# Input split in place in the first block; the first gates in three passes behind the pool projection, with the sample's values between its chunks

## What is computed

```python
z = rms_norm(x) @ w_in   # u 512 | q 512 | k 256 | v 256 | qi 256 | ki 64 | wi 4 | gates 2048
a_pool = pool_mixer(u)   # trailing windows 2, 4, 8, 16, per-group map
a_attn = attend(q, the 256 keys of the highest indexer score, their values, rel_bias)
g = sigmoid(gates)
m = g[..., :1024] * (a_pool @ w_pool_proj) + g[..., 1024:] * (a_attn @ w_attn_proj)
h = x + m @ w_out
y = rms_norm(h + (silu(f[..., :2816]) * f[..., 2816:]) @ w_down), f = rms_norm(h) @ w_gate_up
```

## Time and profile before

| | |
|---|---|
| time of the profiled execution, own time | 1810.34 us |
| its span, first to last instruction | 1808.6 us |
| mean granted TensorE clock, share of 2.4 GHz | 0.975 |
| PE busy (matmuls) | 1689.4 us, 93% |
| DVE (VectorE) busy | 767.3 us, 42% |
| ACT (ScalarE) busy | 458.3 us, 25% |
| POOL (GpSimd) busy | 407.0 us, 23% |

### The profile page before, as it was taken

The page is one execution under the profiler, slowest core; times in us unless marked ns, Lnnn a source line. Parts: engine busy times, 40 slices in busy tenths (PEclk is TensorE's granted clock), DMA queues, the critical chain, the costliest instruction groups (busy, mean ns, idle before and its releaser), DMA issues.

```text
span 1808.6 us, 25066 instructions
## 1 busy us (share of the span) xinstructions
PE 1689.4 (93%) x9820; PEld 1407.8 (78%) x9820; DVE 767.3 (42%) x1882; ACT 458.3 (25%) x860; POOL 407.0 (23%) x351
## 2 busy tenths in 40 slices
PE   4998699989999898779999999999999999999997
PEld 2554266646666555568889999999999999999996
DVE  2214899999200455342144443313313313313325
ACT  1213211253112554331133321121121121121113
POOL 3000205411111432011112242232232232232220
PEclk9996899999999899989999999999999999999999
DMA  5500411260111332032221121111111111111002
GB/s 156 113 26 1 153 63 36 79 247 18 35 38 38 140 141 94 13 100 59 66 70 47 60 81 47 47 46 46 46 46 46 46 46 46 46 46 46 0 1 106
DMA packets 114687, 116.91 MB, mean 65 GB/s; under 512 B 17310, under 2 KB 103982, under 8 KB 112557
## 3 DMA queue, kind: packets, MB, share of 16 engines
q1 hardware_dynamic: 102471, 73.74, 13.7%
q0 software_dynamic: 4160, 39.33, 6.5%
q10 hardware_dynamic: 7982, 2.83, 0.6%
HBM read 107.66 MB, written 8.45 MB: 64 GB/s over the span
## 4 chain that ended last, share of the span: by engine, by line
PE 55%; DVE 1%; DMA 1%; ACT 1%; issue 0%; DVEq 0%; ACTq 0%
PE banks L108 52%; PE banks L1538 3%; DMA out_dram<-yo 0%; PE banks L1519 0%; DVE yo L1856 0%; DVE XL L1769 0%; DMA raw<-in_w_in_dram 0%; ACT XH L1682 0%; DVE rinv L1821 0%; ACT junk L1759 0%; ACT hT L1679 0%; ACT sH L1673 0%; PE banks L1615 0%; PE banks L1561 0%; DVE gated L1776 0%
## 5 line engine op out<-in xcount | busy, mean ns | idle before, releaser
L108 PE MATMUL banks<-hnH,wH 128*128 128x344 f32 x1056 | 339.0, 321 | 3.8 <-DVE sg L1830 3.8
L108 PE MATMUL banks<-hnH,wL 128*128 128x344 f32 x1056 | 337.8, 320 | 0.0
L494 PE MATMUL banks<-hT,big 128*128 128x344 f32 x768 | 226.9, 457 | 1.3 <-ACT I L977 0.7
L494 PEld LDWEIGHTS banks<-hT,big 128*128 128x128 f32 x768 | 147.3, 192 | 79.0 <-issue 2.4
L108 PEld LDWEIGHTS banks<-hnH,wH 128*128 128x128 f32 x1056 | 199.4, 189 | 4.4 <-issue 4.3
L1647 POOL TENSOR_TENSOR wL<-w_raw,wH 128x1024 fp32r<-128x1024 f32 (+1 forms) x55 | 155.8, 2851 | 204.2 <-ACT wH L1709 203.9
L108 PEld LDWEIGHTS banks<-hnH,wL 128*128 128x128 f32 x1056 | 199.2, 189 | 0.0
L1844 DVE TENSOR_TENSOR hT<-hT,banks 128x344 f32<-128x344 f32 x264 | 135.2, 513 | 107.1 <-PE banks L108 107.0
L108 PE MATMUL banks<-aH,wH 128*128 128x344 f32 x528 | 169.3, 321 | 1.6 <-DVE hT L1844 1.6
L108 PE MATMUL banks<-aH,wL 128*128 128x344 f32 x528 | 169.7, 321 | 0.0
L108 PE MATMUL banks<-hnL_lo,wH 128*128 128x344 f32 x528 | 169.1, 320 | 0.0
(11 more groups left out here) (287 smaller groups left out, 2621.1 us busy)
## 6 DMA issues: line engine op xcount, KB each, us to landing
w_raw<-in_w_gate_up_dram SPq DMA_DIRECT2D x44, 512.0 KB, 3.9
w_raw<-in_w_down_dram SPq DMA_DIRECT2D x11, 1024.0 KB, 4.9
big<-in_w_in_dram SPq DMA_DIRECT2D x12, 512.0 KB, 3.9
W<-in_x_prompt_dram SPq DMA_DIRECT2D x8, 512.0 KB, 4.5
raw<-in_w_in_dram SPq DMA_DIRECT2D x8, 512.0 KB, 5.0
x_nat<-in_x_prompt_dram SPq DMA_DIRECT2D x8, 512.0 KB, 4.0
raw<-in_w_out_dram SPq DMA_DIRECT2D x8, 512.0 KB, 3.8
out_dram<-yo SPq DMA_DIRECT2D x8, 512.0 KB, 2.6
```

The costliest lines, as they stand in the source:

```text
L108: last = nc.tensor.matmul(out, w_cols(w, k), x_cols(x, k), start=(k == 0 and j == 0), stop=(k == nk - 1 and j == 2))
L494: last = mm(ps[:, bank, 0:CH], big[:, s, k, :], hT[:, k, c * CH:(c + 1) * CH], start=k == 0, stop=k == KD - 1)
```

## The change

- The area `UD` moves next to `hT`. `XH`, the input's high part, replaces `hT` in place, piece by piece; `XL` lies over `UD`. `x_hi` holds a piece's high part for the while. The residual gets an area of its own in the second block.
- PE does all 24 chunks of the pool projection first, then all first gates, in three passes, on slabs that ACT and POOL split (`high_slab`, `low_slab`). POOL splits the first 12 pieces of the input beside the projections, VectorE the last 12 after them.
- The sample's values lie between the projection's chunks 8 to 23, in 16 halves, each of two `rc`; the gather and its ring are in halves.
- VectorE's loops are three: blocks 3, 4, 5; then the sample and block 2; then blocks 6 and 7, with the sample's softmax steps after rounds 18, 22 and 25.
- PE takes `sum_sample_ties` ahead of the cached keys and waits there; the masks of the sample are added as matmuls at the end of the key stage.
- In attention `transpose_probs(n)` comes after `times_values(n - 1)`.
- In the second block the input's split is gone; the first projection slab and two transposes of x come before the first gate slab, and SP's loads are in another order.

```diff
+                pe.wait_ge(sm_step, SM["ties"])
+                pe.wait_ge(upto_made, 1)
+                mm(ps[:, 6, 0:P + 2], same16[:, :, :].rearrange("p b r -> p (b r)"), seq[:, :], start=True, stop=True)
+                mm(ps[:, 6, 256:256 + P + 1], upto16[:, :], seq[:, 0:P + 1], start=True, stop=True).then_inc(sm_made, 1)
                 pe.wait_ge(zq_ready, 1)
                 pe.wait_ge(uq_evac, 6 + 24)
                 pe.wait_ge(stT_evac, 1)
...
+                pe.wait_ge(sm_step, SM["mask"])
+                pe.wait_ge(lanes_made, 10)
+                for j in range(2):
+                    for b4 in range(4):
+                        for g in range(2):
+                            mm(ps[0:32, 2, j:j + 1], ZQ[:, g, j, 32 * b4:32 * b4 + 32], kT[:, g, SEQ + 4 * j + b4:SEQ + 4 * j + b4 + 1],
+                               start=(b4 == 0 and g == 0), stop=False)
+                    mm(ps[0:32, 2, j:j + 1], new_sel[:, j, :], MK[:, P:P + 1], start=False, stop=True)
+                    for c in range(4):
+                        for rc in range(4):
+                            last = mm(ps[32 * rc:32 * rc + 32, 4 + j, c * P:(c + 1) * P], lane_sel[:, j, c, 32 * rc:32 * rc + 32], MK[:, 0:P],
+                                      start=False, stop=c == 3, tile_position=(0, 32 * rc))
                 last.then_inc(S_ready, 1)
...
+                def sample_values(h):
+                    b, s = divmod(h, 2)
+                    j = b // 4
+                    pe.wait_ge(v_in[s], 16 * (b + 1))
+                    if b == 0:
+                        pe.wait_ge(sp_evac, 2)
+                    elif s == 0:
+                        pe.wait_ge(ob_done, b)
+                    for rc in (2 * s, 2 * s + 1):
+                        for c in range(4):
+                            at = (4 * (rc % 2) + c) * 256
+                            last = mm(ps[32 * rc:32 * rc + 32, 7, 0:256], PTs[:, j, c, 32 * rc:32 * rc + 32], v_ring[:, s, at:at + 256],
+                                      start=c == 0, stop=c == 3 and rc > 0, tile_position=(0, 32 * rc))
+                        if rc == 0:
+                            mm(ps[0:32, 7, 0:256], pd[:, 32 * j:32 * j + 32], vN[0:NB, NBLK, :], start=False, stop=True, tile_position=(0, 0))
+                    last.then_inc(v_used, 1)
...
+                transpose_max()
+                beside = {1: transpose_negmax, 3: sum_probs, 5: transpose_sample_probs}
+                for x in range(PROJ):
+                    m, c = divmod(x, NCH)
+                    if c == 0:
+                        pe.wait_ge(small_in[m % 2], 16 * (m // 2 + 1))
+                    if x >= 6:
+                        pe.wait_ge(p_evac, x - 5)
+                    for k in range(4):
+                        last = mm(ps[:, x % 6, 0:CH], small[:, m % 2, k, :], aP[:, k, c * CH:(c + 1) * CH], start=k == 0, stop=k == 3)
+                    last.then_inc(p_ready, 1)
+                    if x in beside:
+                        beside[x]()
+                    if x >= V_FROM:
+                        h = x - V_FROM
+                        if h >= 2 and h % 2 == 0:
+                            sum_sample_heads(h // 2 - 1)
+                        sample_values(h)
+                sum_sample_heads(NB - 1)
...
                 for m in range(KD):
                     s = m % 2
...
+                    pe.wait_ge(slab_lo, m + 1)
                     for c in range(NCH):
...
+                        for a, k in enumerate(G_ORDER):
+                            if m == 0 and a == 0:
+                                pe.wait_ge(xh_done, 4 * (c + 1))
+                            if m == 0 and a >= 4:
+                                pe.wait_ge(xh_done, 4 * (NCH + c) + a - 3)
+                            for j, (w, v) in enumerate((("hi", "hi"), ("hi", "lo"), ("lo", "hi"))):
+                                last = mm(ps[:, x % 6, 0:CH], G_[w][s][:, k * P:(k + 1) * P], X_[v][:, k, chunk(c)],
+                                          start=(a == 0 and j == 0), stop=(a == KD - 1 and j == 2))
...
                     if n and n % 4 == 0:
                         transpose_sums(n // 4 - 1)
                     if n:
                         times_values(n - 1)
-                    if n in VF_AT:
-                        sum_sample_heads(VF_AT.index(n))
-                    if n in V_AT:
-                        sample_values(V_AT.index(n))
+                    transpose_probs(n)
                 times_values(PAIRS - 1)
...
+                pool.wait_ge(S_ready, 1)
+                load_v(0)
+                load_v(1)
+                for u in range(12):
+                    c, k = units[u]
+                    if u == 0:
+                        pool.wait_ge(ap_ready, NG * NCH)
+                    pool.wait_ge(split_hi, u + 1)
+                    gp.tensor_tensor(XL[:, k, chunk(c)], hT[:, k, chunk(c)], f32(x_hi[u % 2]), ALU.subtract).then_inc(split_lo, 1)
+                    if u >= 2:
+                        load_v(u)
+                for h in range(12, 2 * NB):
+                    load_v(h)
+                low_slab(0)
+                low_slab(1)
                 for m in range(KD):
...
+                dve.wait_ge(causal_done, 4)
...
+                    for c, i in enumerate((3, 4, 5)):
+                        count(c, i, cntA[:, c:c + 1])
...
+                    count(0, 2, cntB[:, 32:33])
+                    dve.wait_ge(lane_step, 4 * r + 1)
+                    V.transpose(lane_cntT[:, :], lane_cnt[:, :]).then_inc(lane_step, 1)
+                    dve.wait_ge(lane_step, 4 * r + 2)
+                    V.tensor_reduce(lane_tot[:, :], lane_cntT[:, :].rearrange("p (b r) -> p b r", r=16), AX.X, ALU.add).then_inc(lane_step, 1)
+                    dve.wait_ge(lane_step, 4 * r + 3)
+                    V.tensor_copy(lane_totT[:, :].rearrange("p (b r) -> p b r", r=16),
+                                  lane_tot[:, :].unsqueeze(2).to_broadcast([P, 2, 16])).then_inc(lane_step, 1)
                     dve.wait_ge(lane_step, 4 * r + 4)
                     V.transpose(cntB[:, 0:32], lane_totT[:, :]).then_inc(counted, 1)
-                    dve.wait_ge(counted, 3 * BITS + 4 * (r + 1))
-                    update(LATER, cntB[:, 31:35], bit, 2 * BITS + 1 + 2 * r)
-                settle(LATER, 4 * BITS + 1)
+                    dve.wait_ge(counted, 3 * BITS + 2 * (r + 1))
...
+                sample_step = {18: sample_max, 22: sample_negmax, 25: sample_weights}
+                LAST = slice(5, 7)
+                for r, bit in enumerate(range(BITS - 1, -1, -1)):
+                    for c, i in enumerate((6, 7)):
+                        count(c, i, cntA[:, c:c + 1])
+                    dve.wait_ge(counted, 5 * BITS + 2 * (r + 1))
+                    update(LAST, cntA[:, 0:2], bit, 4 * BITS + 2 + 2 * r)
+                    if r in sample_step:
+                        sample_step[r]()
+                settle(LAST, 6 * BITS + 2)
+                for k, i in ((4, 6), (5, 7)):
+                    to_mask(k, i)
...
+                dve.wait_ge(p_ready, PROJ)
+                for u in range(12, 24):
+                    c, k = units[u]
+                    dve.wait_ge(split_hi, u + 1)
+                    V.tensor_tensor(XL[:, k, chunk(c)], hT[:, k, chunk(c)], f32(x_hi[u % 2]), ALU.subtract).then_inc(split_lo, 1)
...
-                slab(0)
-                slab(1)
...
                     if m < 2:
+                        slab(m)
                         x_tile(m)
...
+                project(0)
+                for m in range(KD):
+                    if m == 0:
+                        for t in transpose_after(0):
+                            transpose_x(t)
+                    gate(m)
+                    if m:
+                        project(m)
+                        for t in transpose_after(m):
+                            transpose_x(t)
...
-                for n, (c, k) in enumerate(order):
-                    A(XH[:, k, chunk(c)], hT[:, k, chunk(c)], ACT.Copy).then_inc(split_hi, 1)
-                    if n == KD:
-                        high_slab(1)
+                high_slab(1)
+                for t in transpose_after(0):
+                    x_out(t)
...
+                def high_x(u):
+                    c, k = units[u]
+                    if u >= 2:
+                        act.wait_ge(xh_done, u - 1)
+                    A(x_hi[u % 2], hT[:, k, chunk(c)], ACT.Copy).then_inc(split_hi, 1)
+                def keep_x(u):
+                    c, k = units[u]
+                    act.wait_ge(split_lo, u + 1)
+                    A(XH[:, k, chunk(c)], f32(x_hi[u % 2]), ACT.Copy).then_inc(xh_done, 1)
...
+                    if 6 <= x < 18:
+                        high_x(x - 6)
+                        if x > 6:
+                            keep_x(x - 7)
+                    if x > V_FROM and x % 2:
+                        own_values((x - V_FROM) // 2)
+                    if x > V_FROM + 1 and x % 2 == 0:
```

(34 more changed lines are left out.)

444 lines of the change are left out of this document (192 added, 252 removed).

## The result

The changed kernel takes **1858.3 us** (median of 4 runs, 1856.07 to 1861.8) against 1810.99 for the kernel before in the same measurement: ratio 1.0259, 95% interval 1.0243 to 1.0274. It is slower by 47.3 us; forecast were 53.

The account below looks back on a forecast made before the run. TensorE, busy for 93% of the span, was taken as the bound. Terms -20.4 + 2.0 + 39.9 + 22.2 + 2.4 + 1.0 + 10 - 7.7 + 4.0 = +53.4 us gave 1864, range 1834 to 1886.

Parts of the forecast that it names:

- the sample's values: Value products between the projections: eight samples take 59.2 us instead of 19.3 at the serial price, +39.9 us.
- wait for the ties: Ahead of the cached keys: PE idles 24.1 us for VectorE's ties, slowed by POOL, where it idled 1.9; +22.2 us.
- low clock after it, masks as narrow products: Key stage: low clock after the ties pause +2.4 us, masks as 32 narrow products for 8 wide ones +1.0.
- the softmax waits: First projections: PE waits 6 us for sample_negmax and 4 us for sample_weights, +10 (4 to 16); sample_max is covered.
- attention, values and head sums aside: Attention: start wait shrinks -2.6, VectorE waits in the transposes go -6.0, last times_values +0.9; sum -7.7 us.
- second block's start: Second block: SP's load order and ACT's split ahead of the x copy delay the first gate slab, +4.0 us (-5 to +6).
- one column group behind each other, then four on the next: Sample's values: products run serially at 0.48 us each, less some 0.4 at each group change; 7.4 us a sample.
- The first rival: Sample's values: the two column groups of a half overlap, a sample costs 3.95 us; 1836 us, chance 0.12.
- The rival with VectorE in time: Ties ahead of the keys: POOL does not hold VectorE's short steps, the wait is 1 us; 1840 us, chance 0.07.
- its two waits, 3.3 and 2.7 us, go: Attention's transposes: with times_values ahead, VectorE has emptied its bank, so PE's waits for it vanish; -6.0 us.
- The rival at 1960: Value stage: narrow products leave PE mostly idle, the clock falls to 1.2 GHz, 59 + 37 us double; chance 0.05.
- the one on the fast side: Value products run beside the projections at no PE cost; under 5.8 us the sum turns negative, at nothing 1805; chance 0.04.

Follow-up runs that it names:

- ties_and_steps: Changed kernel with PE's two ties products moved into the key loop and VectorE's sample softmax steps after rounds 9, 11, 13 instead of 18, 22, 25: 1828.26 us.
- rc_inside: Changed kernel with the value products' columns c outside, the half's two row groups inside, and the new token's product behind all eight: 1838.99 us.
- mixer_late: Changed kernel with one more wait on POOL, so the pool mixer starts only after VectorE has done the sample's ties: 1882.67 us in one run.
- ties_in_keys: Changed kernel with PE's wait and two products for the sample's ties moved from ahead of the keys into the key loop: 1860.5 us.

## Why the prediction was right

The range held the time, and the forecast was 5.7 us too high. Term by term, expected and in the trace of the changed kernel:

| term | forecast | found |
|---|---|---|
| gates in three passes, with the last splits | -18.4 | -18.9 |
| the sample's values | +39.9 | +36.5 |
| wait for the ties | +22.2 | +21.1 |
| low clock after it, masks as narrow products | +3.4 | +4.3 |
| the softmax waits | +10 | +7.2 |
| attention, values and head sums aside | -7.7 | -9.4 |
| second block's start | +4.0 | +1.0 |
| front of the kernel | 0 | +1.9 |

The found ones sum to 43.7 of the 45.5 us. Two costs stand in no row: 2.1 us of low clock behind the softmax wait of 5.8 (6.78 us from 458.85 to 465.63, where ties_and_steps takes 4.73 for the same work), which the prediction put at nothing, and the wait of 1.0 for ACT at L652. They are 3.1 where 1.8 are missing, which is about how well the rows can be told apart. The errors partly cancel: the values, the softmax waits and the second block's start came out 9.2 us cheaper than forecast, and the low clocks, the front and L652 together 5.9 dearer. The last row is no term of the change: VectorE's first loop starts at 188.8 instead of 187.0 because the low clock lasts one indexer item longer, and in the kernels of this study, which are alike up to there, it starts anywhere from 185.2 to 190.3. A term smaller than that can't be read from a run's time, only from its own stage in the trace.

**Values.** The condition under which I called the prediction wrong, a half under 2.5 us, did not occur, but one of my two halves was not serial. The step that failed is "one column group behind each other, then four on the next", with some 0.4 given back where the group changes: where the change is direct it gives back 0.95 us, and where the new token's product stands in it nothing. That made 6.97 instead of 7.4, so the total is near by two errors that partly cancel. The first rival (the groups overlap fully) is what rc_inside made by an edit; in the changed kernel it is half true in one half of two.

**Ties.** Rounds of 2.13 us, as computed; 13 of them in the mixer's 47.7 us at 3.67, where I had 12.5 at 3.81; the ties at 371.3 to 371.8 against 371.0. mixer_late shows the cause. The step was right, but what the prediction did not say, and ties_in_keys showed, is that the wait was no defect of its place. PE's pause ahead of the keys and the 76 us of VectorE behind it are one chain, and a term of the sum is not what its removal brings. The rival with VectorE in time was the only place where I had thought of the removal, and there I let the softmax waits stand as they were.

**Softmax.** 5.83 and 1.36 at the places named; I had 6 and 4. The second term was the mis-sized one. And the prediction gave a low clock to the long pause alone: behind the 5.83 PE was granted 0.69 until 465.6, and that cost 2.1 us more.

**Attention.** -7.7 forecast, -9.4 found; the order's part, +5.1 when put back, was measured at 4.8. Of the reason ("its two waits, 3.3 and 2.7 us, go") only the first half is right: they go, and 5.2 us of waits for VectorE appear in the next line, so that the gain by PE's listed idle time is 0.6 to 0.8 and not 6.0.

**Second block.** The chain was as written, link by link. The low clock was the mis-sized link: it lasted some 1 us into the gates (granted 0.63 from 837 to 839, then full) where the earlier trace rows had 13.77 against 11.34 for the whole slab. There PE had stood still for 14.9 us before the slab; here it had run the projection and a group of transposes from 817.8 to 827.7.

**Clock in the value stage.** The rival at 1960 falls: 1.00 granted from 480 to 577. So does the one on the fast side: the products took 55.8 us, not under 5.8.

## What to carry over

When narrow products share the array by column group, issue them with the group innermost; if a smaller buffer takes groups away, deal the data out anew so that every piece still touches all of them. Before an engine's wait is moved, follow the waiting chain on the other side: where VectorE's own list sets the time, PE's wait only changes its place, until VectorE's steps move too. And a stall at a stage's start is often two lists in a row: after SP's order was mended (4.5 us), PE's order was the next bound, and both together brought 9.3.

## What the runs showed of the hardware

Two column groups one behind the other are neither serial nor parallel. The second group's first product started with the third of the first group's four (2.73 us for eight, with 1.85 for four). The new token's product, 8 rows instead of 128, between them ended that (4.24 with its 0.54), and it overlapped with no neighbour of either group. The Trainium skill (TensorE: Matmul & The Clock Gate, Part 3: Packing small matmuls) has matmuls start and end strictly in program order. By that the second group could at most start with the first one's last product, after 3 x 0.46 us, and the eight would take 3.2; the trace has 2.73 and disagrees.

POOL holds some steps of VectorE to its own end, also one with a single input: the copy of 32 columns took 1.16 us instead of 0.18, and the update of 2 columns 1.77 instead of 0.16, while the long counts beside the same POOL instructions keep their 0.35 and 0.61. Shortness is not what exposes a step. In the 32 rounds three of them were ever held, the copy (L1339, up to 2.4 us), the compare (L1277, up to 1.7) and the update (L1280); the two transposes of 32 columns (0.21) and the sum over 32 columns (0.19) in the same rounds never were. The Trainium skill (GPSIMD Engine Reference, Key points) limits the contention to two-port modes and to two SBUF inputs; the update has two inputs and agrees, for the copy and the compare, with one input each, no run here tells which mode they were in.
